# Gated blocks and state-space gate: weights stand still and 256 tokens move

## What is computed

```python
def rmsnorm(x, gain):
    y = xf * lax.rsqrt(jnp.mean(xf * xf, axis=-1, keepdims=True) + EPS)
    return (y * gain.astype(jnp.float32)).astype(x.dtype)
...
    # end of s5_mixer, y: (1, 256, 1024)
    y = jax.nn.gelu(y).astype(h.dtype)
    y = y * jax.nn.sigmoid(y @ w_glu)
    return y @ w_out
...
def swiglu(h, w_gate, w_up, w_down):
    return (jax.nn.silu(h @ w_gate) * (h @ w_up)) @ w_down
...
    # in each layer, behind the mixer
    h = rmsnorm(x, ffn_pre_gain[i])
    x = x + rmsnorm(swiglu(h, ffn_w_gate[i], ffn_w_up[i], ffn_w_down[i]), ffn_post_gain[i])
```

## Time and profile before

| what | value |
|---|---|
| median of 3 runs | 1271.31 us (1269.29 to 1272.28) |
| profiled execution | 1271.98 us, span 1270.2 us |
| granted TensorE clock, mean | 0.966 |
| PE busy | 1198.8 us, 94%, 7210 matmuls |
| PEld (weight loads) busy | 977.4 us, 77%, 7210 |
| VectorE busy | 799.7 us, 63% |
| ScalarE busy | 592.4 us, 47% |
| GpSimd busy | 123.3 us, 10% |
| HBM read | 175.25 MB, 139 GB/s over the span |

### The profile page before, as it was taken

How to read it: one execution, slowest core, us unless ns; L and a number is a source line. 1 busy time by engine, 2 the same in 40 slices (tenths; PEclk the granted TensorE clock), 3 DMA queues, 4 the chain that set the end, 5 groups by cost and what they waited for, 6 DMA issues and landing times.

```text
span 1270.2 us, 17529 instructions
## 1 busy us (share of the span) xinstructions
PE 1198.8 (94%) x7210; PEld 977.4 (77%) x7210; DVE 799.7 (63%) x1297; ACT 592.4 (47%) x905; POOL 123.3 (10%) x124
## 2 busy tenths in 40 slices
PE   6899889999999999999999999999989798999997
PEld 5756679797788888888867777887867676888785
DVE  4636664443865777554645689577775868555544
ACT  5455323223455565444544565454473435544531
POOL 0403042320000000000000000000421510000000
PEclk9989799998999999998999999999999899999999
DMA  7422011102455455543512365455533044655551
GB/s 281 170 82 100 33 67 34 67 34 81 145 178 183 176 182 172 182 171 137 169 66 84 116 217 181 165 183 185 191 122 134 3 146 137 200 190 184 189 193 55
DMA packets 49377, 177.45 MB, mean 140 GB/s; under 512 B 5616, under 2 KB 6256, under 8 KB 49040
## 3 DMA queue, kind: packets, MB, share of 16 engines
q1 hardware_dynamic: 49296, 176.32, 40.2%
HBM read 175.25 MB, written 1.05 MB: 139 GB/s over the span
## 4 chain that ended last, share of the span: by engine, by line
PE 81%; DVE 10%; ACT 6%; POOL 2%; issue 1%; DMA 0%; SPq 0%; DVEq 0%; ACTq 0%
PE wps L2572 21%; PE wps L2573 20%; PE wps L2574 20%; PE tps L2561 4%; DVE wlo L1746 2%; PE tps L2618 2%; PE tps L2759 2%; PE tps L2777 2%; PE tps L2768 1%; ACT whi L1373 1%; PE tps L2939 1%; PE tps L2871 1%; DVE arena L1971 1%; POOL arena L2465 1%; ACT over L1658 1%
## 5 line engine op out<-in xcount | busy, mean ns | idle before, releaser
L1746 DVE TENSOR_TENSOR wlo<-raw,whi 128x1024 fp32r<-128x1024 f32 (+1 forms) x322 | 388.5, 1232 | 197.6 <-ACT whi L1373 196.4
L2572 PE MATMUL wps<-whi,a_hi 128*128 128x512 f32 (+1 forms) x1008 | 408.0, 405 | 19.4 <-DVE a_lo L1768 8.4
L2574 PE MATMUL wps<-wlo,a_hi 128*128 128x512 f32 (+1 forms) x1008 | 397.2, 394 | 0.0
L2573 PE MATMUL wps<-whi,a_lo 128*128 128x512 f32 (+1 forms) x1008 | 397.2, 394 | 0.0
L1373 ACT ACTIVATE whi<-raw 128x1024 fp32r<-128x1024 f32 (+1 forms) x322 | 325.1, 1050 | 51.9 <-PE wps L2574 51.0
L2572 PEld LDWEIGHTS wps<-whi,a_hi 128*128 128x128 f32 x1008 | 194.1, 193 | 65.3 <-DVE wlo L1746 13.4
L2574 PEld LDWEIGHTS wps<-wlo,a_hi 128*128 128x128 f32 x1008 | 193.0, 192 | 41.3
L2573 PEld LDWEIGHTS wps<-whi,a_lo 128*128 128x128 f32 x1008 | 193.9, 192 | 36.8
L2572 PE MATMUL wps<-whi,f_hi 128*128 128x512 f32 x264 | 104.8, 397 | 0.0
L2574 PE MATMUL wps<-wlo,f_hi 128*128 128x512 f32 x264 | 104.3, 395 | 0.0
L2573 PE MATMUL wps<-whi,f_lo 128*128 128x512 f32 x264 | 104.3, 395 | 0.0
(11 more groups left out here) (382 smaller groups left out, 1405.1 us busy)
## 6 DMA issues: line engine op xcount, KB each, us to landing
raw<-in_w_dn SPq DMA_DIRECT2D x22, 512.0 KB, 3.3
raw<-in_w_0dn SPq DMA_DIRECT2D x22, 512.0 KB, 3.2
raw<-in_w_1dn SPq DMA_DIRECT2D x22, 512.0 KB, 3.3
raw<-in_w_ua SPq DMA_DIRECT2D x20, 512.0 KB, 3.2
raw<-in_w_ub SPq DMA_DIRECT2D x20, 512.0 KB, 3.3
raw<-in_w_0ug SPq DMA_DIRECT2D x20, 512.0 KB, 3.3
raw<-in_w_0uu SPq DMA_DIRECT2D x20, 512.0 KB, 3.3
raw<-in_w_1ug SPq DMA_DIRECT2D x20, 512.0 KB, 3.3
```

The lines of the kernel that those rows point to most:

```text
L1746: V.tensor_tensor(t.wlo[n % NR][:, 0:w], t.raw[n % NR][:, 0:w], t.whi[n % NH][:, 0:w].bitcast(F32), ALU.subtract).then_inc(m.done(s.dve_lo ...
L2572: T.matmul(o, xh, wh, start=first, stop=False)
L2573: T.matmul(o, xl, wh, start=False, stop=False)
L2574: mm = T.matmul(o, xh, wl, start=False, stop=last)
```

## The change

In groups 1 to 4 and the tail of both gated blocks, and in the state-space gate, the roles of the operands are swapped: `turned_product` loads 128x128 of whi or wlo as weights and moves the 256 tokens of a_hi or a_lo. For each k there are four column tiles f with three matmuls each, so a slab has 24 matmuls of 256 columns instead of 12 of 512. Results have channels on the partitions: two column tiles of 256 tokens in a bank. Group 0 stays as it was.

The transposes of these groups go. The norm's factor is now along the free dimension, so it can't be a per-partition scale: `root_row` spreads it once per block over all partitions by two small matmuls into a scratch bank, copied by ScalarE into the buffer of the post gain (`t.row`), whose next load waits for the last reader. Then VectorE scales the gate product (`gate_scale`), ScalarE takes Silu in place (`gate_silu`), VectorE multiplies by the factor again (`gate_again`, put off to the second slab of the next group) and by the up product (`gate_times`), and `gate_parts` makes the halves. For the tail all of these stand right behind `ut`. In the state-space gate `glu_gate` now gives the sigmoid in the layout of y, and `glu` multiplies directly.

```diff
@@ order_of_work @@
+    def turned_stream(name, banks=None):
+        if banks is None:
+            i = wpair[0]
+            wpair[0] ^= 1
+            banks = wps[2 * i:2 * i + 2]
+        for kp in range(4):
+            n = at["use"]
+            assert SLABS[n][0:2] == (name, kp), (SLABS[n], name, kp)
+            while at["split"] <= min(n + LOOK, len(SLABS) - 1):
+                split_next()
+            for k in (2 * kp, 2 * kp + 1):
+                for f in range(4):
+                    emit("turned_product", name, n, k, f, banks[f // 2].name, k == 0 and f % 2 == 0, k == 7,
+                         k % 2 == 1 and f == 3, both_sides(main.tok[k]), banks[f // 2].free if k == 0 else ())
+            used()
+            while soon:
+                soon.pop(0)()
...
@@ swiglu @@
-        for i in range(5):
-            name, dst = f"{l}ug{i}", f"sg{i % 2}"
-            banks = whole(stream(name, 8, main, {(0, 2): lambda b_: second()} if i == 0 else None))
-            for j in range(2):
-                take(dst, name, j, 0, 512, "Silu", banks[j], sg_free[i % 2])
-            up = f"{l}uu{i}"
-            banks = whole(stream(up, 8, main))
-            for j in range(2):
-                emit("gate_up", dst, name, up, j, 0, 512, banks[j].name)
-                banks[j].free = (("gate_up", up, j),)
-            pending.append(lambda i=i, up=up: groups(i, [("gate_up", up, j) for j in range(2)]))
+        def silu(i, name, banks):
+            for m_, b in enumerate(banks):
+                emit("gate_scale", i % 2, name, m_, b.name, root, sg_free[i % 2])
+                b.free = (("gate_scale", name, m_),)
+                emit("gate_silu", i % 2, name, m_)
+        def times_up(i, name, up, banks):
+            for m_, b in enumerate(banks):
+                emit("gate_times", i % 2, name, up, m_, 1 if up == name else m_, b.name)
+                b.free = (("gate_times", up, m_),)
+        def halves(i, up, n):
+            for m_ in range(n):
+                emit("gate_parts", i % 2, up, m_, ffn.name, 4 * i + 2 * m_)
+                ffn.tok[4 * i + 2 * m_] = ffn.tok[4 * i + 2 * m_ + 1] = ("gate_lo", up, m_)
+            sg_free[i % 2] = (("gate_lo", up, n - 1),)
+        name, up = f"{l}ug0", f"{l}uu0"
+        banks = whole(stream(name, 8, main, {(0, 2): lambda b_: second()}))
+        for j in range(2):
+            take("sg0", name, j, 0, 512, "Silu", banks[j], ())
+        b, root = bank(), norm["tok"]
+        emit("root_row", root, b.name, b.free)
+        b.free = (("root_row", root),)
+        banks = whole(stream(up, 8, main))
+        for j in range(2):
+            emit("gate_up", "sg0", name, up, j, 0, 512, banks[j].name)
+            banks[j].free = (("gate_up", up, j),)
+        pending.append(lambda: groups(0, [("gate_up", f"{l}uu0", j) for j in range(2)]))
+        for i in range(1, 5):
+            name, up = f"{l}ug{i}", f"{l}uu{i}"
+            silu(i, name, whole(turned_stream(name)))
+            pending.append(lambda i=i, name=name: [emit("gate_again", i % 2, name, m_) for m_ in range(2)])
+            times_up(i, name, up, whole(turned_stream(up)))
+            pending.append(lambda i=i, up=up: halves(i, up, 2))
         name = f"{l}ut"
-        banks = whole(stream(name, 8, main))
-        for j in range(2):
-            take("sg1", name, j, 0, 256, "Silu", banks[j], sg_free[1])
-            emit("gate_up", "sg1", name, name, j, 256, 256, banks[j].name)
-            banks[j].free = (("gate_up", name, j),)
-        to_acts("sg1", [("gate_up", name, j) for j in range(2)], ffn, 2, k0=20)
+        banks = whole(turned_stream(name))
+        silu(5, name, banks[0:1])
+        emit("gate_again", 1, name, 0)
+        gain_free[0] += (("gate_again", name, 0),)
+        times_up(5, name, name, banks[1:2])
+        halves(5, name, 1)
@@ state-space gate @@
-    sg = [stream("sg0", 8, main, banks=si_banks)]
+    sg = [turned_stream("sg0", si_banks)]
...
-    sg.append(stream("sg1", 8, main, banks=b2))
+    sg.append(turned_stream("sg1", b2))
...
-        for j in range(2):
-            emit("glu_gate", c, j, banks[j].name)
-            banks[j].free = (("glu_gate", c, j),)
-            banks[j].held = False
+        for i in range(2):
+            emit("glu_gate", 2 * c + i, banks[i].name)
+            banks[i].free = (("glu_gate", 2 * c + i),)
+            banks[i].held = False
 
     def gated(kb):
-        b = bank()
-        emit("glu", kb, b.name, b.free)
-        b.free = (("glu_y", kb),)
@@ place @@
+    t.row = t.gain[:, 0:S]
...
+    t.glu = t.h[:, :, :].rearrange("p j (h c) -> p (j h) c", h=2)
@@ scalar_program @@
+    def root_row(r, b, freed):
+        act.wait_ge(*m.at("root_spread", r))
+        activate(t.row, t.bank[b][:, 0:S], ACT.Copy).then_inc(m.done(s.act_out, "root_row", r), 1)
+    def gate_silu(i, name, m_):
+        g = t.sg[i][:, m_, :]
+        act.wait_ge(*m.at("gate_scale", name, m_))
+        activate(g, g, ACT.Silu).then_inc(m.done(s.act_out, "gate_silu", name, m_), 1)
+    def gate_parts(i, up, m_, acts, k):
+        act.wait_ge(*m.at("gate_times", up, m_))
+        activate(t.acts[acts][0][:, k:k + 2, :], by2(t.sg[i][:, m_, :]), ACT.Copy).then_inc(m.done(s.act_out, "gate_hi", up, m_), 1)
+    def glu_gate(kb, b):
+        act.wait_ge(*m.at("grp", f"sg{kb // 2}", kb % 2))
+        activate(t.glu[:, kb, :], t.bank[b][:, :], ACT.Sigmoid).then_inc(m.done(s.act_out, "glu_gate", kb), 1)
@@ vector_program @@
+    def gate_scale(i, name, m_, b, r, free):
+        dve.wait_ge(*m.at("grp", name, m_))
+        dve.wait_ge(*m.at("root_row", r))
+        wait_all(free)
+        V.tensor_tensor(by2(t.sg[i][:, m_, :]), by2(t.bank[b][:, :]), over2(t.row), ALU.mult).then_inc(
+            m.done(s.dve_out, "gate_scale", name, m_), 1)
...
+    def gate_again(i, name, m_):
+        g = by2(t.sg[i][:, m_, :])
+        dve.wait_ge(*m.at("gate_silu", name, m_))
+        V.tensor_tensor(g, g, over2(t.row), ALU.mult).then_inc(m.done(s.dve_out, "gate_again", name, m_), 1)
...
+    def gate_times(i, name, up, m_, side, b):
+        g = t.sg[i][:, m_, :]
+        dve.wait_ge(*m.at("grp", up, side))
+        dve.wait_ge(*m.at("gate_again", name, m_))
+        V.tensor_tensor(g, g, t.bank[b][:, :], ALU.mult).then_inc(m.done(s.dve_out, "gate_times", up, m_), 1)
...
+    def gate_parts(i, up, m_, acts, k):
+        hi, lo = t.acts[acts]
+        dve.wait_ge(*m.at("gate_hi", up, m_))
+        V.tensor_tensor(lo[:, k:k + 2, :], by2(t.sg[i][:, m_, :]), hi[:, k:k + 2, :].bitcast(F32), ALU.subtract).then_inc(
...
-        dve.wait_ge(*m.at("glu_T", kb))
-        V.tensor_tensor(y2, y2, by2(t.bank[b][:, :]), ALU.mult).then_inc(m.done(s.dve_out, "glu_y", kb), 1)
+        dve.wait_ge(*m.at("glu_gate", kb))
+        V.tensor_tensor(y2, y2, by2(t.glu[:, kb, :]), ALU.mult).then_inc(m.done(s.dve_out, "glu_y", kb), 1)
@@ tensor_program @@
+    def turned_product(name, n, k, f, b, first, last, done, ready, freed):
+        w, cols = SLABS[n][2], slice(k % 2 * SLABS[n][2] + f * P, k % 2 * SLABS[n][2] + (f + 1) * P)
+        o = t.bank[b][:, f % 2 * S:(f % 2 + 1) * S]
+        pe.wait_ge(*m.at("lo", n))
+        wait_all(ready)
+        wait_all(freed)
+        wh, wl = t.whi[n % NH][:, cols], t.wlo[n % NR][:, cols]
+        xh, xl = (a[:, k, :] for a in t.acts["a"])
+        T.matmul(o, wh, xh, start=first, stop=False)
+        T.matmul(o, wh, xl, start=False, stop=False)
+        mm = T.matmul(o, wl, xh, start=False, stop=last and f % 2 == 1)
+        if last and f % 2:
...
+    def root_row(r, b, freed):
+        wait_all(freed)
+        pe.wait_ge(*m.at("root", r))
+        for j in range(2):
+            mm = T.matmul(t.bank[b][:, j * P:(j + 1) * P], t.st[:, 2 + j:3 + j].to_broadcast([P, P]), t.con[:, 0:P], start=True, stop=True)
+        mm.then_inc(m.done(s.pe_side, "root_spread", r), 1)
 
-    def glu(kb, b, freed):
-        wait_all(freed)
-        for sub in range(2):
-            for j in range(2):
-                pe.wait_ge(*m.at("glu_gate", kb // 2, j))
-                mm = turn(t.bank[b][:, sub * S + j * P:sub * S + (j + 1) * P], t.h[:, j, (2 * kb + sub) * P:(2 * kb + sub + 1) * P])
-        mm.then_inc(m.done(s.pe_side, "glu_T", kb), 1)
```

More of the change, by code:

```diff
@@ L258, in stream @@
                         yield
+        return banks
+    def turned_stream(name, banks=None):
[15 more added lines that the diff above has]
+                soon.pop(0)()
+            if kp == 1:
+                while pending:
+                    pending.pop(0)()
+            for g in list(background):
+                if next(g, g) is g:
+                    background.remove(g)
+            yield
         return banks
@@ L1265, in by4, with over2 @@
     return ap.rearrange("p (h s) -> p h s", h=4)
+def over2(ap):
+    return ap.unsqueeze(1).to_broadcast([P, 2, S])
 def over4(ap):
@@ L1692, in glu_gate, with glu @@
     @part
-    def glu_gate(c, j, b):
-        act.wait_ge(*m.at("grp", f"sg{c}", j))
```

(30 more changed lines are left out.)

10 lines of the change are left out of this document (7 added, 3 removed).

## The result

The changed kernel took 1277.6 us in the median of 12 runs (1273.13 to 1284.58), the kernel before 1270.48 in the 12 runs beside them (1268.15 to 1277.8). The ratio is 1.0053 with an interval of 1.0032 to 1.0075: **+6.7 us, between 4.1 and 9.5**. The forecast was 1275.5, +4.2. The profiled execution of after has a span of 1277.9 us (its own time 1280.01), against 1270.2 before: +7.7.

A forecast was written before the change was run, and what follows sets the result against it. TensorE's issue rate was taken as the bound in the gated blocks. Terms 10.7 - 7.1 - 3.7 + 0.6 + 3.7 + 0 gave +4.2 us, 1275.5 us against the median of 1271.31; range 1264 to 1289.

The forecast's parts named there:

- Slabs: Gated blocks, groups 1 to 4 and tail: 72 slabs at 2.87 us, 119.5 ns a matmul, +10.7 us on PE.
- Rival A: Turned matmuls: weight loads set the pace at 111.7 ns, no fixed part paid; kernel 1262 us; 15%.
- rival B: Turned matmuls: load and column paths both full, any slip shows; up to 132.5 ns, kernel 1298, halfway 1287; 16%.
- Transposes of groups 1 to 4: Gated blocks of both layers: these transposes go, 0.89 us of PE a group, -7.1 us.
- tail: Between ut and the down product: four transposes and their wait on ScalarE and VectorE go, -3.7 us.
- The +0.6 charged for the third down slab: Layer 0's down product: the tail's new chain and a VectorE table step delay the third slab's halves, +0.6 us.
- Root wait: Behind ug0: PE waits for the norm's root at root_row, 3.4 and 1.5 us, part given back, +3.7 together.
- VectorE and ScalarE: Groups of the gated blocks: added scale steps are covered by the lookahead, wlo 2.3 us ahead; nothing.
- State-space gate: Slabs +1.2 us, sixteen transposes -1.8, but PE arrives earlier and waits longer for wlo: 0, ends -1.5 to +1.
- Rival C: Behind layer 0's new root wait: granted clock falls to half, +1.6 us, 1277; a third of a chance inside other cases.
- Rival D: Turned matmuls: load and product run in turn, 171 us more, kernel 1446; 1%.
- Rival E: Turned matmuls: two in a row share weights, so a load could be dropped; the forecast or towards rival A.

The follow-up runs named there:

- experiment 3: The kernel before with each 512-column product of groups 1 to 4 and ut issued as two of 256, operand roles kept: 1280.49 us, ratio 1.0066.
- experiment 4: The kernel before without the transposes of groups 1 to 4 and the tail, nothing turned, so other numbers are multiplied: 1261.26 us, ratio 0.991.
- experiment 5: The kernel before with only ut turned and root_row in the second slab of uu0: 1270.86 us, ratio 0.999.
- experiment 2: The kernel before, nothing turned, with root_row's matmuls added behind ug0 and their product unused: 1275.87 us, ratio 1.0033.
- experiment 1: The changed kernel with root_row moved from behind ug0 to the second slab of uu0: 1276.15 us, ratio to before 1.0026.
- experiment 7: The kernel of experiment 1 with the state-space gate as in the kernel before: 1272.6 us, ratio to before 1.0017.
- experiment 8: The kernel of experiment 1 without gate_scale and gate_again, the root's factor left out: 1273.64 us, ratio to before 1.0009.
- experiment 10: The kernel before with ut's transposes put off to the down product's second slab and the state-space gate turned: 1269.37 us, ratio 0.9995.

## Why the prediction was right, and where it was off

The range holds the result, and the forecast case is the one that came: TensorE's issue rate decides, transposes are cheaper than the columns' halving. The size was 2.5 us short in the medians (+6.7 for +4.2), and 2.4 in the two blocks of the trace (+6.6). That the block lengths and the medians come so near to each other is in part luck, since the medians' interval is 5 us wide. By the prediction's steps, with the sizes in the two blocks:

1. **Slabs: forecast +10.7, measured +11.5.** 2.88 for 2.87 us against 2.72, times 72. The choice of 119.5 was half a nanosecond low, 0.8 us in all; the fixed 13.3 ns of the 512-column matmul, which was one of the ends weighed, is the one that holds: (256 / 2.4) + 13.3 = 120.0. Rival A needed less than 117 and rival B more than 122; experiment 3 shows that neither depends on the operands' roles. The Trainium skill (TensorE: Matmul & The Clock Gate, Back-to-back issue gap) gives N/2.4 + 2.5 ns as the gap of a matmul by itself, 109.2 at 256 columns, and for a stream in which each matmul has a weight load 131 ns at 512. The trace agrees with neither (120.0 and 226.7). The prediction worked with the first alone, though this kernel's stream is of the second kind.
2. **Transposes of groups 1 to 4: forecast -7.1**, and
3. **tail: -3.7.** Together -10.7 in experiment 4, as forecast. From the table above the tail alone is 1.91 in layer 0 and 1.63 in layer 1 (ut's stretch, with 0.64 paid for its slabs and 0.89 for group 4's transposes), -3.5 for -3.7, and PE passes from ut to the down product with nothing between. The two ends:

```profile
879.93 0.28 PE L2693 MATMUL wps<-a_hi,wlo 128*128 128x256 f32 x1
880.05 0.40 PE L2671 MATMUL wps<-whi,f_hi 128*128 128x512 f32 x1
...
1207.36 0.28 PE L2693 MATMUL wps<-a_hi,wlo 128*128 128x256 f32 x1
1207.47 0.40 PE L2671 MATMUL wps<-whi,f_hi 128*128 128x512 f32 x1
```

   The +0.6 charged for the third down slab in layer 0 didn't come. VectorE's timeline of after shows the chain of six steps (four are on VectorE) running 3.7 us past ut's end, and the slab's wlo behind it:

```profile
879.53 0.69 DVE L2205 TENSOR_TENSOR h<-wps,gain 128x512 f32<-128x512 f32 x1 [2.10 <-PE wps L2693]
880.92 0.69 DVE L2212 TENSOR_TENSOR h<-h,gain 128x512 f32<-128x512 f32 x1 [0.70 <-ACT h L1756]
881.71 0.69 DVE L2219 TENSOR_TENSOR h<-h,wps 128x512 f32<-128x512 f32 x1
883.10 0.69 DVE L2225 TENSOR_TENSOR f_lo<-h,f_hi 128x512 fp32r<-128x512 f32 x1 [0.70 <-ACT f_hi L1761]
884.05 1.23 DVE L1817 TENSOR_TENSOR wlo<-raw,whi 128x1024 fp32r<-128x1024 f32 x1 [0.26 <-ACT whi L1428]
```

   It ends at 885.28, 5.2 us behind ut's end, 0.4 ahead of its use. The term named the right place: in experiment 5 the wait is there.
4. **Root wait: forecast +3.7, measured +4.4 in experiment 2 and about +4.1 in after.** In layer 0 uu0 starts 3.80 us behind where ug0's issues end in after (753.87 plus three matmuls, to 758.35), of which 0.4 is the clock, so 3.4 as forecast; experiment 2, at full clock there, has 3.56. In layer 1 it is 1.84 (1089.43 plus three matmuls, to 1091.95) and 1.86 in experiment 2, where 1.5 was forecast, and there the term was mis-sized: in both executions ug0 of layer 1 ran in part at half clock, and the root was written 1.3 us behind its end, not 1.08 (1.3 in the six traces of this document with such a stretch there, 1.1 in the six without). From the root to the product it is 0.52 us instead of 0.4, and uu0 itself became 0.1 longer in each layer by its restart. The 1.2 to be given back in layer 0 was right: in experiment 2 uu0 needs 0.72 less with its restart (11.72 to 11.00) and ug1 with uu1 0.4 less (24.16 to 23.75), 1.1 together.
5. **VectorE and ScalarE: forecast nothing, measured +0.3 in after and 1.4 without the root's wait.** The lookahead of 2.3 us was read in layer 1, where it holds (2.0 left). In layer 0, at uu1, gate_scale stands behind the tables, and wlo comes late: PE loses 0.30 us in after, though it comes late itself from the root's wait. Take that wait away and 1.4 us of the price shows (experiments 1, 7 and 8). The prediction named this as a sign that it is wrong (wlo becomes what PE waits for inside the blocks, and is no longer ready over 1 us ahead), and in layer 0 the sign came, at one of eight ends. Its size is too small to move the forecast. It asked what covers the steps, and took layer 1's cover for both layers.
6. **State-space gate: forecast 0, measured about +0.15 (experiment 10).** The mechanism is in part as forecast: PE arrives earlier, as the transposes go, and waits longer, in after too. PE's timeline in the output product, for the earlier trace rows:

```profile
1055.48 0.47 PE L2671 MATMUL wps<-whi,a_hi 128*128 128x512 f32 x1 [0.97 <-DVE a_lo L2463]
1058.86 0.50 PE L2671 MATMUL wps<-whi,a_hi 128*128 128x512 f32 x1 [0.42 <-DVE wlo L1817]
```

   It is the gated product's lo half that PE waits for first, 0.97 us; the wait for wlo that was named is as long as before (0.42 for 0.41).

**Rival C, the clock, came, and is the largest part of what the sum lacks in the blocks.** Windows of after behind the root's wait in layer 0, and behind the ordinary wait ahead of ug0 in layer 1, and then of experiment 2 behind the root's wait in layer 0:

```profile
757.50:760.50 3.00, 3.00 (x9) 2.61 (x10) 2.00 (x10) 2.65 (x5) 0.00 (x0) 0.50 0.55 216
```

```profile
1078.00:1081.00 3.00, 3.00 (x8) 2.32 (x8) 2.58 (x16) 0.00 (x0) 0.00 (x0) 0.50 0.00 1
```

```profile
754.50:757.50 3.00, 3.00 (x16) 2.54 (x16) 2.00 (x10) 2.84 (x5) 0.00 (x0) 1.00 0.31 124
```

The first two are at 0.50, 1.2 GHz. In layer 0 the stretch costs about 1.4 us: 0.4 at root_row, and 1.0 in uu0, which became 0.29 longer though 0.84 of waiting and restart ahead of ug1 went. In layer 1 it costs 0.6: ug0 took 13.51 us up to the end of its issues for 12.90 before. And the stretch behind ug0's wait in layer 0, which before had the earlier trace rows, is absent in after, though the wait ahead of it is the same 2.30 us; that returns 0.65 (13.50 to 12.85). The prediction set the twelve matmuls of the earlier trace rows at 4.27 for 2.72 us; in after the same twelve took 2.84 at full clock, and over half of the difference went into a wait behind them. Experiment 2 has a longer root wait in layer 0 (2.93 us) than after, and the clock behind it is 1.00. So whether the clock falls there belongs to the execution and not to the change, as far as these traces show.

The sum with these sizes: slabs 11.5, transposes -7.1, tail -3.5, root waits 3.4 + 1.8 + 0.2 for the restarts, given back -0.8 ahead of ug1 and -0.5 behind it, VectorE 0.3, clock 1.4 + 0.6 - 0.65: some +6.6, and 6.6 was measured in the blocks. (The -0.5 is what the table leaves in layer 0 from ug1 to ut when the other terms are taken off; no experiment gives it by itself.) Without the clock's 1.4 it is +5.3, 1.1 over the forecast: slabs 0.8, the root's wait 0.4, the tail 0.2, VectorE 0.3, less the 0.6 charged for the third down slab. For experiment 1, with 0.9 for root_row's two calls in place of the root waits, 0.7 given back in layer 0, 1.4 for VectorE and the same clock as before: 11.5 - 7.1 - 3.5 + 0.9 - 0.7 + 1.4 = +2.5, against 2.5. How much of the runs' median of +6.7 is clock stays open; the blocks' +5.3 without it is inside the interval too.

Rivals D and E are out by the spacing and by the count of loads.

## What to carry to other kernels

A matmul here costs its columns plus some 13 ns, so turning a product to spare its transposes is a purchase: twice the matmuls at half the columns cost 1.28 us a group of eight slabs, the transposes saved 0.89. Before a transpose at the end of a stage is removed, ask when its result is needed: putting it into the next product's second slab got most of the tail's gain for one line, 2.9 of 3.5 us by its trace. A small instruction put into the bound engine's queue is priced by what it waits for, and whatever that wait was covering comes due when it is mended. A cover that was read in one layer has to be read in the other too, if another queue is fuller there.
